# Odd layer's rotary embedding: the exchanged halves brought by DMAs inside SBUF, with signed sines, in place of a permutation product on TensorE

## What is computed

```python
def rope(t):
    ...
    t1, t2 = tf[..., : d // 2], tf[..., d // 2:]
    return jnp.concatenate([t1 * cos - t2 * sin, t1 * sin + t2 * cos], axis=-1)

def odd_mixer(x, w_in, lam_p, subln_g, w_out, lam_init):
    q, k, v = jnp.split(x @ w_in, 3, axis=-1)
    q = rope(q.reshape(B_, S, 16, 64)); k = rope(k.reshape(B_, S, 16, 64))
    ...
    o = diff_attention(q, k, v, lam)
    return (rms_norm(o, subln_g) * (1.0 - lam_init)).reshape(B_, S, 1024) @ w_out
```

## Time and profile before

| | |
|---|---|
| median of 3 runs | 2343.31 us |
| the profiled execution, its own time | 2339.33 us |
| its span in the trace | 2337.5 us |
| mean granted TensorE clock | 0.988 |
| PE, DVE, ACT, POOL busy | 96%, 62%, 45%, 5% |
| odd layer's rotations and attention | from about 490 to 590 us of the span |

### The profile page before, as it was taken

The page is one execution under the profiler, slowest core; times in us unless marked ns, Lnnn a source line. Parts: engine busy times, 40 slices in busy tenths (PEclk is TensorE's granted clock), DMA queues, the critical chain, the costliest instruction groups (busy, mean ns, idle before and its releaser), DMA issues. The chain is left out here.

```text
span 2337.5 us, 38028 instructions
## 1 busy us (share of the span) xinstructions
PE 2247.8 (96%) x15963; PEld 2068.8 (89%) x15963; DVE 1453.4 (62%) x1708; ACT 1055.1 (45%) x1239; POOL 116.7 (5%) x179
## 2 busy tenths in 40 slices
PE   8989999998999999999999998999999999998998
PEld 7868899887898998998998987998998997987996
DVE  6676555568756556566765676556456865676454
ACT  3534444445344443443555444444443545444442
POOL 2140000000000000000011000000000002000000
PEclk9999999999999999999999999999999999999999
DMA  8546556643445565666642664565656543564553
GB/s 245 171 143 199 163 165 197 224 145 109 164 161 168 194 221 176 199 200 193 189 153 76 202 211 137 186 202 191 196 188 204 183 151 110 187 227 146 166 187 117
DMA packets 337753, 411.68 MB, mean 176 GB/s; under 512 B 11244, under 2 KB 269480, under 8 KB 337456
## 3 DMA queue, kind: packets, MB, share of 16 engines
q1 hardware_dynamic: 328480, 377.18, 49.8%
q0 software_dynamic: 9104, 32.06, 4.5%
HBM read 406.31 MB, written 5.00 MB: 176 GB/s over the span
## 5 line engine op out<-in xcount | busy, mean ns | idle before, releaser
L1581 DVE TENSOR_TENSOR wl<-raw,wh 128x2048 fp32r<-128x2048 f32 (+2 forms) x351 | 763.7, 2181 | 563.7 <-ACT wh L1115 467.9
L345 PE MATMUL bank<-xl,wh 128*128 128x256 f32 x3136 | 875.4, 279 | 8.4 <-DVE xl L1614 4.1
L345 PE MATMUL bank<-xh,wl 128*128 128x256 f32 x3136 | 869.5, 277 | 0.0
L345 PE MATMUL bank<-xh,wh 128*128 128x256 f32 x3136 | 869.5, 277 | 0.0
L1115 ACT ACTIVATE wh<-raw 128x2048 fp32r<-128x2048 f32 (+2 forms) x351 | 637.3, 1822 | 332.0 <-PE bank L345 291.2
L345 PEld LDWEIGHTS bank<-xl,wh 128*128 128x128 f32 x3136 | 591.8, 189 | 17.5 <-issue 16.6
L345 PEld LDWEIGHTS bank<-xh,wl 128*128 128x128 f32 x3136 | 590.7, 188 | 0.5 <-issue 0.2
L345 PEld LDWEIGHTS bank<-xh,wh 128*128 128x128 f32 x3136 | 590.9, 188 | 0.0
L345 PE MATMUL bank<-wl,hh 128*128 128x512 f32 x528 | 205.9, 390 | 0.0
L345 PE MATMUL bank<-wh,hh 128*128 128x512 f32 x528 | 205.5, 389 | 0.0
L345 PE MATMUL bank<-wh,hl 128*128 128x512 f32 x528 | 205.5, 389 | 0.0
(11 more groups left out here) (372 smaller groups left out, 3165.8 us busy)
## 6 DMA issues: line engine op xcount, KB each, us to landing
raw<-in_ffn_w_in SPq DMA_DIRECT2D x80, 1024.0 KB, 5.2
raw<-in_w_mix_in SPq DMA_DIRECT2D x56, 1024.0 KB, 5.3
raw<-in_ffn_w_gu SPq DMA_DIRECT2D x40, 1024.0 KB, 5.2
raw<-in_ffn_w_out SPq DMA_DIRECT2D x40, 1024.0 KB, 5.1
raw<-in_ffn_w_down SPq DMA_DIRECT2D x20, 1024.0 KB, 5.1
raw<-in_mem_wkv SPq DMA_DIRECT2D x16, 1024.0 KB, 5.9
raw<-in_even_w_in SPq DMA_DIRECT2D x14, 1024.0 KB, 8.1
raw<-in_odd_w_in SPq DMA_DIRECT2D x12, 1024.0 KB, 5.3
```

The lines of the kernel that those rows point to most:

```text
L345: ins = pe.transpose(o, a, b) if transpose else pe.matmul(o, a, b, start=start, stop=stop)
L1581: dve.tensor_tensor(part_of(t, 1), raw_tile(t), part_of(t, 0).bitcast(F32), ALU.subtract)\
```

## The change

- PE: all eight `rotate(i)` go, and with them the use of the `acc` ring by them.
- POOL: in `odd`, after its two loads, for each tile four DMAs of 32 partitions x 512 float32 (64 KB each) from `rs` to a new half of `rt`. Partition block q receives block q ^ 1. They wait for ACT's copy of that tile, and from i = 2 on also for `rope_done` of tile i-2.
- DVE: `rope(k)` multiplies `rs` by cosine first, then waits for `rotated{k % 2}`, multiplies the exchanged copy by sine, and adds. It no longer calls `get(("rot", k))`.
- The minus sign of the first half moves into the sine table. `oc` shrinks from 640 to 512 columns, `rt` grows from 3 to 4 x 512.

```diff
-    c["sin"] = np.tile(np.sin(ang), (4, 1))
+    c["sin"] = np.tile(np.sin(ang), (4, 1)) * np.where(i % 64 < 32, -1.0, 1.0)[:, None]
...
@@ PE, odd
-            def rotate(i):
-                await_read(("rp", i))
-                if i == 0:
-                    pe.wait_ge(sig("odd_loaded"), 16)
-                o = take(("rot", i), "acc")
-                mm(o[:, :], oc[:, 0:P], rs[:, i % 2, :], True, True, ("rot", i))
...
             rope_tile(0)
             rope_tile(1)
-            rotate(0)
             rope_tile(2)
-            rotate(1)
...
-                if t + 2 < 8:
-                    rotate(t + 2)
...
@@ DVE, odd
             def rope(k):
-                name = ("rot", k)
                 ahead(("rp", k))
-                o = get(name)
                 n = ROPE_ORDER[k]
                 if k == 0:
                     wait("odd_loaded", 16)
                 else:
                     wait("rope_done", k)
-                free(name, dve.tensor_tensor(two(rt[:, 0, :]), two(o[:, :]), sin, ALU.mult))
-                link(dve.tensor_tensor(two(rt[:, 1, :]), two(rs[:, k % 2, :]), cos, ALU.mult))
-                await_read(name)
+                dve.wait_ge(bank_free[where[("rp", k)][0]], where[("rp", k)][3])
+                dve.tensor_tensor(two(rt[:, 1, :]), two(rs[:, k % 2, :]), cos, ALU.mult)
+                wait(f"rotated{k % 2}", 64 * (k // 2 + 1))
+                link(dve.tensor_tensor(two(rt[:, 0, :]), two(rt[:, 2 + k % 2, :]), sin, ALU.mult))
                 dve.tensor_tensor(rq[:, 2 * n:2 * n + 2, :], two(rt[:, 0, :]), two(rt[:, 1, :]), ALU.add)\
                    .then_inc(sig("rope_done"), 1)
...
@@ POOL, odd
-            const(oc[:, :], "rot", 640, "odd_loaded")
+            const(oc[:, :], "cos", 512, "odd_loaded")
...
+            for i in range(8):
+                if i >= 2:
+                    pool.wait_ge(sig("rope_done"), i - 1)
+                await_read(("rp", i))
+                for q in range(4):
+                    dst, src = 32 * q, 32 * (q ^ 1)
+                    pool.dma_start(rt[dst:dst + 32, 2 + i % 2, :], rs[src:src + 32, i % 2, :])\
+                        .then_inc(sig(f"rotated{i % 2}"), 16)
```

More of the change, by code:

```diff
@@ L40 @@
 for _name, _w in (("ident", 128), ("tri_le", 128), ("tri_ge", 128), ("na_mask", 256), ("causal_le", 128),
-                  ("causal_ge", 128), ("rot", 128), ("cos", 256), ("sin", 256), ("topk_causal", 384),
+                  ("causal_ge", 128), ("cos", 256), ("sin", 256), ("topk_causal", 384),
                   ("strict", 384), ("strict_neg", 384), ("bucket", 512)):
@@ L58, in shape_constants @@
     c["causal_ge"] = np.where(i[None, :] >= i[:, None], 0.0, NEG)
[L59 to L65, removed]
     inv = np.float32(10000.0) ** (-np.arange(0, 64, 2, dtype=np.float32) / np.float32(64))
@@ L180, in program @@
     st = ExitStack()
-    oc = sb("oc", [P, 640], F32, st)
+    oc = sb("oc", [P, 512], F32, st)
     rq = sb("rq", [P, 16, S], F32, st)
-    rt = sb("rt", [P, 3, 512], F32, st)
+    rt = sb("rt", [P, 4, 512], F32, st)
     rs = sb("rs", [P, 2, 512], F32, st)
@@ L1967, in odd @@
                                    1.0 - LAM_INIT, None, ALU.mult))
-            cos = oc[:, 128:384].unsqueeze(1).broadcast_to([P, 2, S])
-            sin = oc[:, 384:640].unsqueeze(1).broadcast_to([P, 2, S])
+            cos = oc[:, 0:256].unsqueeze(1).broadcast_to([P, 2, S])
+            sin = oc[:, 256:512].unsqueeze(1).broadcast_to([P, 2, S])
             def rope(k):
-                name = ("rot", k)
                 ahead(("rp", k))
-                o = get(name)
                 n = ROPE_ORDER[k]
```

## The result

The changed kernel takes 2353.51 us (median of 5 runs, 2351.86 to 2358.39) against 2343.31 us (5 runs, 2338.62 to 2351.0). The ratio is 1.0044, its 95% interval 1.0023 to 1.0065: slower by 10.2 us. That is clear of the noise, since the interval leaves out 1, and it is just under the 0.5% (11.7 us) that the prediction took as the bound of "no change". The forecast was 2342.6 in a range of 2335 to 2352. The time lies just outside that range, and on the side away from the forecast.

The account below looks back on a forecast made before the run. DVE was taken to bound the loop, at 8.75 us of work per 8.98 us unit, with transfers mostly hidden. Early stalls were made up and 0.23 us gained per late unit: -0.7 us, 2343.31 to 2342.6, range 2335 to 2352.

Parts of the forecast that it names:

- T: In the odd layer, time from the end of ACT's copy to the last transfer's landing; taken as 4.3 us.
- Rival 3: Transfers decide the odd layer's pace: at T = 7.8 together about +10 us, 2353; chance 0.15.
- The upper bound of the prediction, T = 7.8: Transfer chain with issue of 0.63 us three times and the slowest landing beside weight loads, 5.8 us.
- 11.4 + T: Loop from projection end through copy, transfer, rope, normalisation, transposes and scores, spanning two units: 15.7 us, 7.9 per unit.
- one long idle time of PE: PE idle 4.0 us ahead of the first scores, then 3.4 us at half pace, losing 1.7 us of work.
- the sum of -0.7 us: Net effect of the odd layer's steps, 0.6 to 0.7 us early at unit 6: 2343.31 becomes 2342.6.
- The steps: Odd layer, rope by rope: rope 3 stalls 1.9 us, rope 5 0.8, ropes 4, 6 and 7 none.
- Rival 1: PE sets the pace in the odd layer, so the whole 7.7 us comes: 2335.6; chance 0.07.
- rival 4: DVE holds POOL's issues: +3 us, 2346, chance 0.08; all four of a tile held: 2370, chance 0.03.
- late weight loads: Transfers beside the odd layer's weight loads cost nothing; were loads late, splits would be, stretching a unit by as much.

Follow-up runs that it names:

- traffic: The kernel before plus 32 transfers of the same size from `oc` to spare columns of `rt`, awaited by nobody but POOL: 2344.21 us, ratio 0.9998.
- late: The changed kernel with the rope of tile t+2 behind the normalisation of unit t-1 on DVE: 2351.11 us, one run.
- hold_late: The changed kernel with the edits of both `hold` and `late`: 2342.43 us, ratio 0.9999 to the kernel before.
- nowait: The changed kernel without its 32 transfers and the wait for them, the sine multiplying `rs` itself: 2335.14 us, ratio 0.9963 to the kernel before.
- actq: The changed kernel with each tile's four transfers issued by ACT behind its own copy, not by POOL: 2357.58 us, ratio 1.0049 to the kernel before.
- warm: The changed kernel with eight unused products of the old size back on PE at their old places: 2358.7 us, one run.
- hold_split_late: `hold_late` with the first two splits back ahead of ropes 0 and 1: 2342.75 us, ratio 1.0002 to the kernel before.
- hold: The changed kernel with SP holding back, from tile 3 on, the nearby weight load until the tile's transfers landed: 2347.57 us, ratio 1.0014 to the kernel before.
- half: The changed kernel with transfers of 32 x 256, the sine multiplying the first 256 columns twice: 2357.76 us, one run.
- poolcopy: The changed kernel with POOL copying the four 32 x 512 blocks itself instead of issuing DMAs: 2343.89 us, ratio 1.0004 to the kernel before.

## Why the prediction was wrong

**Right.** The products left PE. PE stood idle 3.74 us ahead of the first scores (about 4 forecast), and the clock was at 1.2 GHz for 3.4 us behind it, as after the idle times of the earlier trace rows. Issues took 0.50 us, under the 0.62 of the earlier trace rows. Alone, a tile's exchange takes T = 3.8 to 4.4 us, against 4.3 taken from the earlier trace rows. Rope 0 waited 3.60 us. DVE's work in a unit with O is 8.78 us, forecast 8.75. Rival 3 had the right cause, transfers that land late beside weight loads, with a chance of 0.15. That its price of about +10, 2353, is also the measured time is luck: its 3.5 us at rope 0 did not come, and the rest does not lie evenly on six units but in units 1, 3 and 5.

**The step that failed** is the term T of the transfer chain, and in it this sentence: "I lean on the quiet value because weight loads of this stage start when a split ends, two or more us after the tile's copy". In the kernel after, the split ends 0.5 and 0.4 us after the copy (525.64 and 526.16; 547.67 and 548.05), and T is 8.3 us in place of 4.3.

The two us were not in the kernel before either. In the earlier trace rows the copy of tile 6 ends at 544.27, and in the earlier trace rows the split ends at 545.51. The load that it frees is issued at once, as the tile `raw` on SP shows in the kernel before (window 543:549 us):

```profile
L2427 SPq DMA_DIRECT2D raw<-in_odd_w_out x1: 368/368/368, 545.6 to 545.6; - x1
```

From the copies of tiles 3 to 7 to these loads it is 1.3 to 1.7 us, while the fourth transfer is issued about 2 us behind the copy. `traffic` has that order, and its tile 3 takes 7.8 us. The upper bound of the prediction, T = 7.8, was the value to lean on even without a look at the new order.

With T = 8.3 in place of 4.3 the chain written there, 11.4 + T, is 19.7 for two units. But that form spreads a delay over both units, and here it was not spread: one rope takes all of it, 6.02 us, and during that stall the next tile's copy and transfer go by unseen (tile 4's landed at about 536.5, and rope 4 came at 541.75). Hence 14.45 and 8.02 us, 22.5 for the two, instead of 19.7, and stalls of 6.0, 5.6 and 2.7 us in ropes 3, 5 and 7 where 1.9, 0.8 and none were forecast.

**Missed with it**: the two low stretches of the clock behind those stalls. The prediction looked for one long idle time of PE, at the start of the loop; a late rope makes another, because what stands behind the wait on DVE is the normalisation that PE needs. That the order there was a cost of its own `late` and `hold_late` showed.

**The gain was sized about rightly**, though the sum of -0.7 us hides it. The steps have 9.3 us from rope 3 to rope 4 (522.2 to 531.5), 1.9 of them stall, and 7.4 from rope 4 to rope 5 (538.9); `nowait` has 7.40 and 7.42. Units 0 to 2 fell from 8.54 to 7.41 us there, 3.4 us in all, and units 3 to 5 (8.98, 8.91, 8.80 to 8.78) by the little that the earlier trace rows allow. The -7.6 of `nowait` is not to be set against the -0.7: its first maxima come 3.5 us earlier than those of the kernel after (27.22 us into the stage against 30.68), since rope 0 has no exchange to wait for. Rival 1, "the whole 7.7 comes", was right in size if the exchange were free, though not for its reason: DVE, not PE, set the pace of `nowait`.

**Nothing came of** POOL's issues held by DVE (rival 4), or of late weight loads: in `traffic` they land 0.7 us later in the median, and its stage is 0.3 us longer. Nor was it POOL's queue: `actq` is as slow as the change.

**Open**: how much of the loss is PE at 1.2 GHz, beyond the bounds given above; why the large load goes ahead of the small transfers in the DMA engines; and whether another cover for rope 0 would make `hold_late` measurably faster than the kernel before. None of this was tried beyond `warm` and `hold_split_late`.

## What to carry to other kernels

A small transfer on a path that someone waits for is to be costed by what runs beside it when it starts, and in a periodic loop that is the same thing every time: look for the event that frees the large load's buffer and set its time against that of the small transfer, in the order of the changed kernel. A transfer's wait belongs behind the work that another engine stands for. And 32 partitions moved by an engine's own copy (four times 0.59 us on ACT) are shorter and steadier than a trip by DMA, if that engine has 2.4 us to give.

## What the runs showed of the hardware

- **A 64 KB transfer inside SBUF lands in 1.9 to 2.0 us alone, as tiles 4 and 6 of the kernel after do, and in 4.1 to 6.3 when a 1 MB load is issued at the same time** (tiles 3, 5 and 7). From ACT's queue it is 4.7 to 5.9 at tile 3. Not every lone landing is quick: one of tile 3's four took 3.5 in `hold`, with no load beside it. While the load ran, the small one's queue stood. The queue view of the kernel after, window 529.4 to 530.5 us (packets, MB, share of the 16 engines), then 530.5 to 532:

```profile
q1 hardware_dynamic: 203, 0.42, 105.6%
q0 software_dynamic: 5, 0.00, 0.3%
...
q0 software_dynamic: 93, 0.19, 44.8%
q1 hardware_dynamic: 132, 0.24, 44.0%
```

  The first of tile 3's four transfers moved its packets up to 529.5; the other three went from 530.9 on, as the load ended, though all had been issued by 528.1. "DMA: Bandwidth & Descriptors" in the Trainium skill, section "Queues, rings and completion order", has each engine take turns between the queues that have work, packet by packet, and a packet there is a bundle of about 9 to 17 descriptors, 64 at most. What the profile counts as packets are pieces of 2 KB (0.42 MB in 203), 12.7 of them for each of 16 engines in the first window. That may be one turn of such a bundle, so the window can't tell whether there are turns; it shows that three small transfers stood for 1.1 us or more.
- **Half the size helps less than by half**: 32 KB transfers still took up to 5.2 us beside a load, and 1.7 alone (`half`).
- **An ACT copy of 32 partitions takes as long as one of 128**: 0.588 and 0.597 us for 512 columns. POOL's copy of 32 x 512 took 0.604 to 2.792 us (`poolcopy`), and a multiplication on DVE beside the first of them 1.08 in place of 0.69.
- **An issue on ACT takes 0.51 to 0.62 us of ACT's time** (`actq`), with one of 1.55, against 0.50 on POOL.
- **Idle times of PE of 3.74, 5.47 and 4.35 us stood with 3.4, 6.8 and 6.8 us at 1.2 GHz** in the kernel after. The second and third low stretches began before the idle time was over, in stalls that were not forecast. One of 1.51 us ahead of 580.26 had no such stretch.
